# The out projection's first panel waits for the mixed tile block by block

## What is computed

```python
# gated DeltaNet (layers 0 and 3)
o = rms_norm(o, norm_g) * jax.nn.silu(z...)
out = o.reshape(b, t, D_MODEL).astype(h.dtype) @ w_out
# short convolution (layer 1)
return (bg * conv_centred(cg * u, conv_w)) @ w_out
# attention (layer 2)
return merge_heads(o).astype(h.dtype) @ w_out
```

## Time and profile before

| | |
|---|---|
| median of 3 runs | 2341.35 us (2337.91 to 2343.45) |
| profiled execution | 2342.44 us, span 2340.6 us |
| granted TensorE clock, mean | 0.981 |
| TensorE busy | 2231.0 us, 95% of the span |
| VectorE, ScalarE busy | 482.0 us (21%), 391.8 us (17%) |
| moved by DMA | 550.93 MB, mean 235 GB/s |

### The profile page before, as it was taken

How to read it: one execution, slowest core, us unless ns; L and a number is a source line. 1 busy time by engine, 2 the same in 40 slices (tenths; PEclk the granted TensorE clock), 3 DMA queues, 4 the chain that set the end, 5 groups by cost and what they waited for, 6 DMA issues and landing times.

```text
span 2340.6 us, 44306 instructions
## 1 busy us (share of the span) xinstructions
PE 2231.0 (95%) x19787; PEld 1662.4 (71%) x19787; DVE 482.0 (21%) x1352; ACT 391.8 (17%) x795; POOL 67.1 (3%) x109
## 2 busy tenths in 40 slices
PE   6999998999999999999998999999998989999998
PEld 4776666888888756646676588888878867466465
DVE  2334432000111400000212320002344423000002
ACT  1133223100110100000113220002143331000001
POOL 3000001000000000000000000000000000000000
PEclk8999999999999999999999899999999999999999
DMA  8967889753346499999774696413440047999992
GB/s 328 272 240 289 300 314 274 226 156 107 125 144 215 143 376 386 384 380 378 283 233 170 228 276 182 136 37 111 141 144 7 12 145 251 383 387 381 380 382 113
DMA packets 355911, 550.93 MB, mean 235 GB/s; under 512 B 11280, under 2 KB 311184, under 8 KB 343232
## 3 DMA queue, kind: packets, MB, share of 16 engines
q1 hardware_dynamic: 344352, 525.31, 64.7%
q0 software_dynamic: 5840, 18.11, 3.0%
q10 hardware_dynamic: 5536, 4.73, 0.6%
HBM read 537.64 MB, written 14.93 MB: 236 GB/s over the span
## 4 chain that ended last, share of the span: by engine, by line
PE 78%; SPq 10%; DVE 5%; ACT 2%; DMA 2%; issue 2%; ACTq 0%; DVEq 0%
PE ps L643 76%; SPq L483 7%; SPq L487 3%; ACT ring L1445 2%; DMA ring<-in_moe_w_down 1%; DVE ring L1997 1%; ACT work L1445 1%; DVE ring L2015 0%; DVE work L1856 0%; DVE ring L2020 0%; DVE ring L2005 0%; DMA ring<-in_ada_w 0%; PE ps L1141 0%; PE ps L1034 0%; DVE ring L2023 0%
## 5 line engine op out<-in xcount | busy, mean ns | idle before, releaser
L643 PE MATMUL ps<-hT,ring 128*128 128x256 f32 x3200 | 714.0, 382 | 3.4 <-DVE hT L1866 3.2
L643 PE MATMUL ps<-ring,work 128*32 128x384 f32 (+7 forms) x8008 | 692.0, 436 | 22.4 <-DMA ring<-in_moe_w_gu 5.4
L643 PEld LDWEIGHTS ps<-hT,ring 128*128 128x128 f32 x3200 | 609.0, 191 | 113.1 <-issue 12.2
L643 PEld LDWEIGHTS ps<-ring,work 128*32 128x32 f32 (+2 forms) x8008 | 390.9, 114 | 302.2 <-issue 178.6
L1445 ACT ACTIVATE work<-ps 128x256 f32<-128x256 f32 (+6 forms) x220 | 100.7, 468 | 1331.4 <-PE ps L643 1152.4
L643 PE MATMUL ps<-work,ring 128*128 128x256 f32 (+1 forms) x1344 | 288.0, 374 | 10.6 <-DVE work L2082 6.0
L643 PEld LDWEIGHTS ps<-work,ring 128*128 128x128 f32 (+1 forms) x1344 | 241.7, 187 | 46.4 <-DVE work L2082 7.7
L643 PEld LDWEIGHTS ps<-ring 64*64 64x64 f32 x4192 | 160.5, 139 | 59.3 <-ACT ring L1445 24.2
L643 PE MATMUL ps<-ring 64*64 64x64 f32 (+1 forms) x4192 | 182.7, 230 | 19.8 <-ACT ring L1445 7.2
L1445 ACT ACTIVATE ring<-ps 128x512 f32<-128x512 f32 (+3 forms) x208 | 101.7, 492 | 341.4 <-PE ps L643 330.4
L643 PE MATMUL ps<-work 128*128 128x128 f32 (+2 forms) x736 | 107.4, 297 | 4.7 <-DVE work L2202 4.6
(11 more groups left out here) (260 smaller groups left out, 933.6 us busy)
## 6 DMA issues: line engine op xcount, KB each, us to landing
ring<-in_moe_w_gu SPq DMA_DIRECT2D x96, 1536.0 KB, 16.0
ring<-in_ada_w SPq DMA_DIRECT2D x96, 1024.0 KB, 7.0
ring<-in_moe_w_down SPq DMA_DIRECT2D x48, 1536.0 KB, 16.4
ring<-in_ff_w_gu SPq DMA_DIRECT2D x88, 512.0 KB, 6.1
ring<-in_dn_w_in SPq DMA_DIRECT2D x32, 1024.0 KB, 5.6
ring<-in_moe_w_gu SPq DMA_DIRECT2D x32, 1024.0 KB, 9.1
ring<-in_ff_w_down SPq DMA_DIRECT2D x44, 512.0 KB, 7.2
ring<-in_moe_w_down SPq DMA_DIRECT2D x32, 512.0 KB, 11.6
```

The lines of the kernel that those rows point to most:

```text
L643: return pe.matmul(out, lhsT, rhs, start=start, stop=stop, **kw)
```

## The change

The waits for the whole mixed tile go. `project` gets a function that is called before each matmul of the first column half; for the first out-projection panel this waits, in the attention layer, for block k, and in the other layers, before every second block, for the pair of blocks. The second half needs no waits, as all blocks are then there. In the short convolution a wait for ScalarE's eighth copy of the layer takes the place of the old one: that copy reads bank 0, which the first out-projection panel writes.

```diff
-            def project(n, b, rhs, s=None, between=None):
+            def project(n, b, rhs, s=None, between=None, mixed=None):
...
+                        if mixed and c == 0:
+                            mixed(k)
                         ins = mm(ps[:, b, c * NT:(c + 1) * NT], w[:, k, c * P:(c + 1) * P], rhs[:, k, :],
                                  k == 0, k == KC - 1)
...
             def out_proj(l):
+                def mixed(k):
+                    if KIND[l] == "na":
+                        pe.wait_ge(a_mix, k + 1)
+                    elif k % 2 == 0:
+                        pe.wait_ge(d_mix, MIX0[l] + k // 2 + 1)
+
                 pe.wait_ge(d_ar, ada_turned[0])
                 for i in range(4):
                     if i >= 2:
                         pe.wait_ge(d_x, 8 * l + i - 1)
-                    project(PLAN.first[l]["out"][i], i % 2, mixT)
+                    project(PLAN.first[l]["out"][i], i % 2, mixT, mixed=mixed if i == 0 else None)
...
-                pe.wait_ge(d_mix, MIX0[l] + 4)
 
             def shortconv(l):
...
-                pe.wait_ge(d_mix, MIX0[l] + 4)
+                pe.wait_ge(a_pj, PJ0[l] + 8)
...
-                pe.wait_ge(a_mix, KC)
```

## The result

The changed kernel takes 2326.73 us (median of 6 runs, 2323.13 to 2331.08), against 2340.94 us (6 runs) of the kernel before beside it: ratio 0.9932, 95% interval 0.9922 to 0.9943. A second measurement gave 2325.64 us and the same ratio, 0.9932 (0.9913 to 0.9951). That is 15.9 us by the ratio, 13.3 to 18.3 by the first interval and 11.5 to 20.4 by the second, and 14.2 us between the first two medians. The forecast was 13.2 us, so by time alone it was missed narrowly. The profiled execution has a span of 2325.0 us, 15.6 less than before.

The account below looks back on a forecast made before the run. TensorE, 78% of the chain of waits, was taken to bound the kernel; 8.20 us of waits plus 4.98 us of clock, 13.18 us off the 2341.35 median, gave 2328.2 us, range 2325.2 to 2336.5.

Parts of the forecast that it names:

- What bounds the kernel: TensorE holds 78% of the chain of waits; savings at the four out projections reach the end, as expert stretches shift whole.
- The time that is waited: Matmuls done early before the first out-projection panels: 2.59 us in layers 0, 1 and 3, 0.43 in layer 2; 8.20 us.
- The clock: Shorter idle time before the panels of layers 0, 1 and 3 avoids three falls of TensorE's clock: 4.98 us.
- The rule of the Trainium skill: Frequent short idle times between matmul groups make the clock swing; by it the clock's part is 0, the sum 8.20 us.
- What else the change adds: 20 waits instead of 4 in the first panels, taken at 0 us; no DMA added, TensorE's order unchanged.
- The 1.0 us kept for the range: Upper bound for the added waits in the first panels: 20 x 0.05 us.
- The sum: Waits 8.20 plus clock 4.98 give 13.18 us, taken off the median of 2341.35: 2328.2 us.
- the four places: The starts of the first out-projection panels in layers 0 to 3, where the whole forecast saving of 13.18 us arises.
- the forecast less 3: Low end of the range, 2325.2 us; a median may be off by 1 to 3 us.
- rival 1: At the first panels the clock falls as before, so only 8.20 us are saved: 2333.2 us; chance 0.22.
- rival 2: DMA-bound expert stretches hold their end times, so only layer 2's 0.43 us is left: 2340.9 us; chance 0.08.
- Rival 3: Low clock begun in mid-panel grows into longer stretches, making the kernel slower: 2346 us and more; chance 0.04.

Follow-up runs that it names:

- the fillers alone: Kernel before, with six idle identity matmuls put into TensorE's waits for the whole tile in layers 0, 1 and 3: ratio 0.9967, 7.7 us faster.
- The shifted kernels: Idle matmuls between layer 2's first two out-projection panels: 1, 3, 5 on the kernel before, 3 on the changed; L2-L3 536.28, 537.16, 536.29, 537.26 us.
- the shifted changed kernel: Changed kernel with three idle identity matmuls between layer 2's first two out-projection panels: 537.26 us from layer 2's first residual to layer 3's last product.
- the delay: Changed kernel with 16 more identity matmuls between layer 1's first and second out-projection panels: 2336.95 us, ratio 0.9979 to the kernel before.
- the shift of five matmuls: Kernel before with five idle identity matmuls between layer 2's first two out-projection panels: 536.29 us from layer 2's first residual to layer 3's last product.

## Why the prediction was right and where it fell short

- **What bounds the kernel, and that nothing behind stands still:** right. L0-L1 moved whole, the sync queue's waits kept their lengths, and 16 matmuls put ahead of the DMA-bound stretch were not absorbed.
- **The time that is waited:** right. 2.59 us a place was forecast, 7.28 - 4.68 = 2.60 measured. Layer 2 gave 0.54 instead of 0.43: the panel now starts 0.32 us behind the start of the last values' records (1344.12 to 1344.44 us) instead of 0.85 (1352.02 to 1352.87), so the start after a wait was saved too. In layers 0 and 3 0.26 us of idle time stayed, not 0.42: from the last sum's end (373.16 us in layer 0) the six matmuls take 2.75 us with the whole length of the last record, not 2.59.
- **The clock:** right in layers 1 and 3, in size and reason; in layer 0 right by the number, with the reason not settled. 1.62 and 1.68 us a fall were forecast; the fillers alone gave 1.56, 1.68 and 1.69. That the six matmuls and what is left of the idle time hold the clock is shown by the rows at 1.00. But all nine profiles with the new wait or fillers in layer 0 have a low clock in the sums or, in the kernel with the DeltaNet layers' change alone, from the last sum into the panel, and the three of the kernel before have none there. The code up to the sums is the same, so where that low clock stood is luck, and it took 0.84 us back. One support of the forecast was luck too: 3.10 us of idle time in layer 2 kept the clock in the kernel before, but behind the same idle time it fell in three later profiles (place 2 took 8.54, 8.69 and 9.75 us). The rule of the Trainium skill that was set against it (TensorE: Matmul & The Clock Gate, "A second HAM failure mode: psum-queue depth-cycling") would have left 8.20 us; the traces give 13.3, so here the measurement decides against it.
- **What else the change adds:** right, nothing, tested with 256 waits. The 1.0 us kept for the range was not needed.
- **The sum:** this is the step that failed, by what it left out. It added the four places (13.18 forecast, 13.31 in the traces) and took the rest of the program as unchanged. By the ratio 15.9 us were gained, which is 2325.4 us from the median of before on record and 2325.0 from the second one, just inside and just under the range's low end of 2325.2; the measured median, 2326.73, lies inside. The runs show clock falls outside the places in place of that nothing: 2.0 us for one fall between layers 2 and 3 that came in all three profiles of the kernel before and in none of the three of the changed one, and 1.5 us in the routing of layer 1, where low clock filled 6.8 to 13.6 us before and 6.8 after. The three profiles of each kernel are 17.0 us apart on average; places, this fall and the routing make 16.9, and what is left (the stretch up to layer 0 0.5 us longer, the expert stretch and the end some 0.3 us shorter each) cancels nearly. The prediction looked at the clock only where an instruction was changed, though the trace of before had the fall at 1640.7 to be seen. It could have seen that a fall stood there, not that it would vanish: the shifted kernels show that this hangs on a few microseconds. What is open is why the falls repeat three times of three in one kernel, and which stretch gave the attention's change alone 3.5 us; its one profile lacks the fall in L2-L3, which is 2.0 of them.
- **The range:** "the forecast less 3" allowed for a median's scatter but not for clock falls that appear or vanish far away. The fall in L2-L3 alone is 2.0 us, and in the shifted changed kernel places 2 and 3 and L2-L3 were 3.8 us longer beyond the shift.
- **The rivals:** rival 1 is out by the clock rows and the fillers, rival 2 by the delay. Rival 3 did not come, but low stretches do grow: the changed kernel with three idle matmuls has one of 6.8 us that it has not without them.

## What to carry to other kernels

An idle time of a few microseconds before a dense stretch on TensorE is worth more than its length when the clock falls behind it: here, in layers 1 and 3, 2.6 us of work in the wait and 1.7 us of clock. Wait for the pieces of an input instead of for the whole, and count the matmuls that really fit between the last instruction ahead in the queue and the last piece; in layer 2 eight waits had room for one. A change that moves everything behind it by some microseconds should be given 2 to 4 us either way for clock falls elsewhere (an estimate from the 2.0 and 3.8 us seen here), and the trace should be searched for falls near narrow or sparse work.

## What the runs showed of the hardware

- The clock fell with TensorE busy without a gap, behind 3.65 us of 128x32 matmuls (granted 0.50 from 1640.7 to 1644.0 us). The fall was gone when everything behind layer 2's first panel stood 2.16 us later, and it came in the changed kernel when that stood 1.29 us later.
- About 3.0 us of idle time before layer 0's panel lost the clock in seven of nine profiles with the old wait, but not in two: place 0 took 7.27 us instead of 8.9 in the kernel with the short convolution changed and in the one with the shift of five matmuls, whose code is unchanged up to there. In both a low clock of 3.4 us stood in the sums just ahead; in two of the seven it stood there too. The Trainium skill (TensorE: Matmul & The Clock Gate, "Part 1: The HAM clock gate") says that the watching runs freely and isn't set by the kernel's start; these two profiles agree. 2.77 us lost it in the one profile that had such a gap, 1.47 us in none of eight.
- Adding matmuls can leave a stretch as long as it was: 536.28 us with one, 536.29 us with five.
